# Transposing 64 sample rows with a 64x64 corner of the identity in a hybrid decoder step

## What is computed

```python
h = rmsnorm(x, norm1_g)
xa, ga, q, k, v, gate_a, gate_b = jnp.split(jnp.einsum('btd,de->bte', h, w_in), IN_SPLITS, axis=-1)
...
q = rmsnorm(q.reshape(shp), q_norm_g[:, None, :])
k = rmsnorm(k.reshape(shp), k_norm_g[:, None, :])
...
x = x + jnp.einsum('btd,de->bte', merged, w_out)
h2 = rmsnorm(x, norm2_g)
```

## Time and profile before

| what | value |
|---|---|
| median of three runs | 1177.57 us (1176.91 to 1178.87) |
| profiled execution, its own time | 1177.21 us |
| its span, first to last instruction | 1175.4 us |
| TensorE products (PE) | 1169.3 us busy, 8973 instructions |
| TensorE weight loads (PEld) | 1132.5 us busy, 8973 |
| VectorE (DVE) | 653.1 us |
| ScalarE (ACT) | 454.7 us |
| GpSimd (POOL) | 167.4 us |

### The profile page before, as it was taken

The page is one execution under the profiler, slowest core; times in us unless marked ns, Lnnn a source line. Parts: engine busy times, 40 slices in busy tenths (PEclk is TensorE's granted clock), DMA queues, the critical chain, the costliest instruction groups (busy, mean ns, idle before and its releaser), DMA issues.

```text
span 1175.4 us, 21565 instructions
## 1 busy us (share of the span) xinstructions
PE 1169.3 (99%) x8973; PEld 1132.5 (96%) x8973; DVE 653.1 (56%) x1329; ACT 454.7 (39%) x714; POOL 167.4 (14%) x261
## 2 busy tenths in 40 slices
PE   9999999999999999999999999999999999999998
PEld 7998998998999999999999999999999999999998
DVE  6653533633622255666645558887337885378741
ACT  6444444443433357676533444222112222122221
POOL 2374153252330000000100120000000000000000
PEclk9999999999999999999999999999999999999999
DMA  8576255354331222231262222322323223232332
GB/s 241 153 209 165 79 139 149 96 144 128 108 102 54 76 83 72 73 90 55 84 176 78 71 83 80 88 81 81 95 72 89 77 83 91 75 89 72 89 99 60
DMA packets 183493, 118.52 MB, mean 101 GB/s; under 512 B 7114, under 2 KB 175694, under 8 KB 183418
## 3 DMA queue, kind: packets, MB, share of 16 engines
q1 hardware_dynamic: 172352, 89.47, 26.7%
q0 software_dynamic: 11056, 28.01, 8.6%
q10 hardware_dynamic: 10, 0.01, 0.0%
HBM read 107.43 MB, written 8.45 MB: 99 GB/s over the span
## 4 chain that ended last, share of the span: by engine, by line
PE 99%; DVE 1%; ACT 0%; issue 0%; ACTq 0%; DVEq 0%
PE ps L659 66%; PE ps L638 20%; PE ps L962 2%; PE ps L728 1%; PE ps L715 1%; PE ps L792 1%; PE ps L877 1%; PE ps L796 1%; PE ps L756 1%; PE ps L771 1%; PE ps L740 1%; PE ps L802 1%; PE ps L759 1%; PE ps L681 0%; DVE w_s L1445 0%; PE ps L760 0%
## 5 line engine op out<-in xcount | busy, mean ns | idle before, releaser
L659 PE MATMUL ps<-h,w_s 128*128 128x288 f32 x3840 | 517.6, 296 | 0.0
L659 PEld LDWEIGHTS ps<-h,w_s 128*128 128x128 f32 x3840 | 512.7, 189 | 4.7 <-issue 4.7
L1439 DVE TENSOR_TENSOR w_s<-w_raw,w_s 128x1024 fp32r<-128x1024 f32 (+1 forms) x160 | 193.8, 1211 | 187.7 <-ACT w_s L1048 187.6
L1048 ACT ACTIVATE w_s<-w_raw 128x1024 fp32r<-128x1024 f32 (+1 forms) x160 | 166.2, 1039 | 333.9 <-PE ps L659 328.1
L638 PE MATMUL ps<-w_s,h 128*128 128x384 f32 x1152 | 217.6, 341 | 0.9 <-DVE w_s L1445 0.5
L638 PEld LDWEIGHTS ps<-w_s,h 128*128 128x128 f32 x1152 | 198.7, 188 | 4.6 <-issue 2.4
L659 PE MATMUL ps<-g_hi,w_s 128*128 128x288 f32 x672 | 119.1, 297 | 0.0
L659 PEld LDWEIGHTS ps<-g_hi,w_s 128*128 128x128 f32 x672 | 99.3, 189 | 0.0
L659 PE MATMUL ps<-g_lo,w_s 128*128 128x288 f32 x336 | 71.9, 296 | 0.0
L600 POOL DMA_DIRECT2D out<-f_row x6 | 3.4, 568 | 415.1 <-ACT f_row L1393 415.1
L659 PEld LDWEIGHTS ps<-g_lo,w_s 128*128 128x128 f32 x336 | 54.1, 189 | 0.0
(11 more groups left out here) (299 smaller groups left out, 1433.3 us busy)
## 6 DMA issues: line engine op xcount, KB each, us to landing
w_raw<-in_w_in SPq DMA_DIRECT2D x65, 512.0 KB, 3.9
w_raw<-in_w_up SPq DMA_DIRECT2D x48, 512.0 KB, 4.0
w_raw<-in_w_down SPq DMA_DIRECT2D x24, 512.0 KB, 3.7
kc<-in_cache_k_g POOLq DMA_DIRECT2D x48, 128.0 KB, 3.3
vc<-in_cache_v_g POOLq DMA_DIRECT2D x12, 512.0 KB, 6.4
w_raw<-in_w_out SPq DMA_DIRECT2D x8, 512.0 KB, 3.7
w_raw<-in_w_br_a SPq DMA_DIRECT2D x7, 512.0 KB, 3.9
x_tok<-in_x_prompt SPq DMA_DIRECT2D x4, 512.0 KB, 7.6
```

The source lines that it names most:

```text
L659: last = mm(pu[u % 2][:, 512 * a:512 * a + HALF], w[:, part, k, :], x[:, k, HALF * a:HALF * (a + 1)], start=(k == 0 and i == 0), stop=(k = ...
L1048: A(w_s[:, ring(u), 0, 0:nkt[u], :], w_raw[:, u % NRAW, 0:nkt[u], :], ACT.Copy).then_inc(hi_ready, 1)
L1439: TT(w_s[:, ring(u), 1, 0:nkt[u], :], w_raw[:, u % NRAW, 0:nkt[u], :], w_s[:, ring(u), 0, 0:nkt[u], :], ALU.subtract).then_inc(lo_ready, 1)
```

## The change

The sample's transposes at L716 and L916 take only the 64 rows that hold tokens, with the 64x64 corner of the identity, and write 64 columns instead of 128. GpSimd's memset of the slot in `x_tok2` and its semaphore go, since the rows it zeroed are no longer read. Nothing else is changed.

```diff
-            pool.memset(x_tok2[1][:, 1, :], 0.0).then_inc(x2_pad, 1)
-            pool.wait_ge(x2_pad, 1)
             pool.dma_start(x_tok2[1][0:NS, 1, :], x_srows).then_inc(x2_in, 16)
...
-                tr(TQ[:, SEQ + g * P:SEQ + (g + 1) * P], buf[:, NCLS, g, :], ident).then_inc(tq_ps, 1)
+                tr(TQ[:, SEQ + g * P:SEQ + g * P + NS], buf[0:NS, NCLS, g, :], ident[0:NS, 0:NS]).then_inc(tq_ps, 1)
...
-                tr(ps[3][:, SEQ:SEQ + P], x_tok2[1][:, 1, c * P:(c + 1) * P], ident).then_inc(x2_ps, 1)
+                tr(ps[3][:, SEQ:TOK], x_tok2[1][0:NS, 1, c * P:(c + 1) * P], ident[0:NS, 0:NS]).then_inc(x2_ps, 1)
```

More of the change, by code:

```diff
@@ L336, in build @@
         sga_rdy, mg_rdy, mg_hi_rdy, mg_lo_rdy = (sem(x) for x in ("sga_rdy", "mg_rdy", "mg_hi_rdy", "mg_lo_rdy"))
-        x2_in, x2_ps, x2_cp, sq2_rdy, sq_added, sq2_hi_rdy, sq2_lo_rdy, sq2_used, x2_pad = (sem(x) for x in (
-            "x2_in", "x2_ps", "x2_cp", "sq2_rdy", "sq_added", "sq2_hi_rdy", "sq2_lo_rdy", "sq2_used", "x2_pad"))
+        x2_in, x2_ps, x2_cp, sq2_rdy, sq_added, sq2_hi_rdy, sq2_lo_rdy, sq2_used = (sem(x) for x in (
+            "x2_in", "x2_ps", "x2_cp", "sq2_rdy", "sq_added", "sq2_hi_rdy", "sq2_lo_rdy", "sq2_used"))
         ones_rdy = sem("ones_rdy")
```

## The result

The changed kernel takes 1186.44 us in the median of six runs (1185.82 to 1187.50), the kernel before 1177.95 in its six (1176.91 to 1178.87). The ratio is 1.0072, 95% interval 1.0062 to 1.0082: 8.5 us slower. The profiled execution took 1185.84 us.

What follows compares the result with a forecast made beforehand. TensorE, busy 1169.3 of 1175.4 us, was taken to bound the kernel. 16 x 0.29 + 16 x 0.28 = +9.1 us on 1177.2 gave 1186.3, or 1186.7 on the median's footing; forecast 1186.6, range 1182.0 to 1189.0.

Steps and rivals of the forecast that it cites:

- The bound: Whole kernel: TensorE is busy 1169.3 of 1175.4 us, so hardly any wait could absorb added TensorE time.
- The price of a change of rows: At each lone 64-row transpose, loads and products come late going there and back: 0.34 us in all.
- (a): At the load before L716: no stall, only the shorter product counts, -1.5 us, 1176.1 us; chance 0.05.
- (b): Stall only between product and short transpose, not between two transposes: +1.4 us, 1179.0 us; chance 0.05.
- (c): One of the two changes at each single short transpose is hidden: +4.8 us, 1182.4 us; chance 0.09.
- (d): Shorter product's gain lost and a bank or reader adds: 0.35 to 0.40 a place, 1189 to 1190 us; chance 0.05.
- The size: Over the 32 places at L716 and L916: +0.29 us at 16, +0.28 at 16, sum +9.1 us.
- The saving of the shorter product: Each of the 32 sample transposes moves 64 identity columns, not 128: 0.047 us saved each, 1.5 us in all.
- GpSimd's memset: Losing this 0.99 us memset issues the sample's DMA 1.3 us sooner, over 60 us before its reader: gain nothing.
- Drain and hidden loads: On TensorE: the skill's mode-change drain holds for 64 rows, not 64-column stationaries; its rule against overlapping full loads contradicts the trace.
- two drains of 128 cycles: Estimate from the skill's drain figure at each of 32 places: 0.107 us per place, +1.9 us instead of +9.1.

Runs made afterwards that it cites:

- in a row: Changed kernel with each of the 24 short key and query transposes issued twice, directly one after the other: 1187.96 us.
- apart: Changed kernel with each short key and query transpose issued a second time between the second and third prompt transpose of its group: 1194.30 us.
- grouped: Changed kernel with the three short transposes of a key or query visit together behind its twelve prompt transposes: 1181.52 us.
- the run of the output stage alone: Kernel before with only the transposes of the input's second copy (L916) made short and the memset removed: 1180.29 us, +2.3 us.

## Why the prediction was right

**The bound.** Right. TensorE had no slack: visits longer by 8.5 us in sum, runs longer by 8.5. Nothing was absorbed and nothing new waited.

**The price of a change of rows.** Right in its mechanism: the load comes late on the way there and on the way back, and is no longer hidden. One reading in it was off. The prediction has loads "otherwise follow at 0.17" and so the load 0.09 late; the rows show that a load otherwise starts together with the instruction in front of it, so it is 0.26 late there and 0.20 late in the key visit. The 0.09 are what the start of the instruction itself loses. The sum is not touched, since it was taken from starts of instructions over whole visits. The runs with the transposes in a row, apart and grouped show that the change is what is paid for, and those with 72 and 96 rows that it is tied to having 64 rows and not to being short. Rivals (a) and (b) fall: there is a stall, and it is there between two transposes. So does (c), since a single short transpose pays both ways, and (d), since no place costs 0.35.

**The size.** One term was too large. I took 0.34 for every place, read from visits that lie between products. In front of a product it holds: 0.29 net in the output stage, 2.3 us over its eight. Between transposes the way back is cheaper: the second full transpose comes only 0.06 late (0.17 behind the first instead of 0.11), where the second product comes 0.11 late. Such a place, one short transpose with its way in and back, costs 0.24 net, as the key visit shows: 0.77 - 0.29 = 0.48 for its two inner ones. With that, 16 x 0.24 + 16 x 0.29 = 8.5 instead of my 9.1. 1186.6 was forecast and 1186.4 came. That closeness is partly luck: the term was 0.6 us too large, and the median of before had meanwhile risen from 1177.57 to 1177.95. The difference, 9.1 against 8.5, is the fairer measure.

**The saving of the shorter product.** 0.047 each was counted inside the net price, and can't be seen by itself there. Where it stands alone, with 72 rows, only half of it comes: 0.6 us over all, none in front of products.

**GpSimd's memset.** Right: the page of the profile after has one GpSimd instruction fewer, and the run of the output stage alone costs what its eight changes cost.

**Drain and hidden loads.** The Trainium skill, TensorEngine Tiling, Key Properties, says that a change of tiling mode drains TensorE. For the rows the runs here agree that such a change has a price: to 64 rows and back from them the step is 0.20 us instead of 0.11, with 72, 96 and 120 rows no step is longer. That it is a drain, no run shows. For columns the prediction went too far. The transposes with a 64-column stationary operand show no gap, but whether they run as narrow tiles at all is not shown. Products that are no transposes and take 32 columns (L756, in the attention) do show it in the kernel before:

```profile
91.56 0.49 PE L774 MATMUL ps<-const,prob 128*64 128x128 f32 x3
...
91.98 0.16 PEld L756 LDWEIGHTS ps<-kT,qT 128*32 128x32 f32 x8 [0.20 <-issue]
92.55 0.30 PEld L759 LDWEIGHTS ps<-kT,qT 128*128 128x128 f32 x2 [0.41 <-issue]
```

Their load starts 0.20 us behind the start of the transpose in front (91.56 + 0.49 - 0.27 = 91.78), as at a change to 64 rows, and the full load behind them sat idle for 0.41; both come 16 times. How much of the 0.41 is the change, no run here separates.

The prediction's estimate of two drains of 128 cycles gave +1.9 us and missed, mostly because it leaves out the load that is no longer hidden. The Trainium skill, TensorE: Matmul & The Clock Gate, Part 3, says that a load overlaps products in flight only in another row group. That does not hold here: full loads ran under full products, and the ones with other rows were those that waited.

**Left open.** Whether 65 to 71 rows behave as 72 do, and whether 64 rows in the upper half of the array would cost the same, was not tried. Nor does any run show what in TensorE makes the load wait.

## What to carry to other kernels

In a stream of instructions on 128 rows, a lone matmul or transpose of 64 rows starts about 0.09 us late, the instruction behind it starts late again, and a weight load is no longer hidden: 0.24 to 0.29 us net for each, far more than its shorter product saves (0.05). Keep such an instruction above 64 rows (72 were enough here; against 128 rows the runs could tell no gain) or put all the short ones together. Judge such a change by start-to-start times at its two edges, not by busy time or by the step inside a long run of equal instructions. In front of a product with a full weight load the shorter transpose saved nothing here.

## What the runs showed that was not expected

A transpose of 72 rows is cheaper than one of 64 when it stands alone (the visit with three of them takes 1.91 us against 2.77), and eight in a row with 72 rows are cheaper than eight with 42 (0.91 against 1.17). The way back to a full transpose costs about 0.05 us less than that to a product. A plain float32 product of this size ran as two pairs of load and product and cost 0.22 us more than the transpose.
